# One level of Strassen in the first product of an MLP, for groups 2 to 7 of 8

## The reference, cut to what matters

```
h = layer_norm(DEEPNORM_ALPHA * h + mixed @ w_out, ln1_g, ln1_b)
f = jnp.square(jax.nn.relu(h @ w_ff1)) @ w_ff2        # w_ff1: 1024 x 4096, w_ff2: 4096 x 1024
h = layer_norm(DEEPNORM_ALPHA * h + f, ln2_g, ln2_b)
```

## Time and profile before

| | |
|---|---|
| median of 3 runs | 698.24 us (698.01 to 699.11) |
| the profiled execution | 697.22 us, its span 695.4 us |
| granted TensorE clock, mean | 0.997 |
| busy share of the span | TensorE 98%, VectorE 52%, GpSimd 49%, ScalarE 38% |
| the MLP's groups from up 1 to down 6 | 321.4 to 657.4 us of the span |

### The profile page before, as it was taken

The page is one execution under the profiler, slowest core; times in us unless marked ns, Lnnn a source line. Parts: engine busy times, 40 slices in busy tenths (PEclk is TensorE's granted clock), DMA queues, the critical chain, the costliest instruction groups (busy, mean ns, idle before and its releaser), DMA issues.

```text
span 695.4 us, 13894 instructions
## 1 busy us (share of the span) xinstructions
PE 682.0 (98%) x5643; PEld 656.1 (94%) x5643; DVE 362.9 (52%) x710; ACT 265.4 (38%) x512; POOL 341.1 (49%) x438
## 2 busy tenths in 40 slices
PE   8999999999999999999999999999999999999996
PEld 5989999999997589999999999999999999999995
DVE  7745646576655546589633524525325335245246
ACT  6866666777656334552222112212112112122112
POOL 4554233444444034407964645545545556455437
PEclk9999999999999999999999999999999999999998
DMA  7362231321448922102232222222222222322303
GB/s 242 100 213 73 82 92 61 91 84 49 137 165 278 345 75 92 62 32 91 90 124 78 83 94 82 91 91 92 91 91 89 95 65 88 94 90 91 122 1 129
DMA packets 34005, 73.66 MB, mean 106 GB/s; under 512 B 3988, under 2 KB 19380, under 8 KB 33942
## 3 DMA queue, kind: packets, MB, share of 16 engines
q1 hardware_dynamic: 26822, 68.88, 30.1%
q10 hardware_dynamic: 6864, 3.90, 1.9%
q0 software_dynamic: 256, 0.00, 0.0%
HBM read 67.16 MB, written 5.60 MB: 105 GB/s over the span
## 4 chain that ended last, share of the span: by engine, by line
PE 89%; DVE 3%; ACT 2%; DMA 2%; SPq 2%; issue 1%; POOL 0%; ACTq 0%; DVEq 0%
PE acc L2000 48%; PE acc L1639 29%; PE o_bank L1747 2%; PE acc L1733 1%; PE t_bank L1733 1%; DMA k_t<-cache_k_b 1%; DMA xin<-x_prompt 1%; PE acc L1763 1%; ACT xin L752 1%; SPq L542 1%; PE s_bank L1723 1%; DMA w_raw<-weights 1%; PE s_bank L1722 1%; PE s_bank L1719 0%; PE s_bank L1720 0%
## 5 line engine op out<-in xcount | busy, mean ns | idle before, releaser
L629 POOL TENSOR_TENSOR w_lo<-w_raw,w_hi 128x256 fp32r<-128x256 f32 x352 | 280.2, 827 | 301.4 <-ACT w_hi L731 301.4
L731 ACT ACTIVATE w_hi<-w_raw 128x1024 fp32r<-128x1024 f32 x88 | 92.9, 1057 | 161.1 <-PE acc L2000 132.5
L1639 PE MATMUL acc<-h_hi,w_hi 128*128 128x288 f32 (+1 forms) x416 | 129.2, 311 | 1.7 <-DVE h_lo L1142 1.1
L1639 PE MATMUL acc<-h_lo,w_hi 128*128 128x288 f32 (+1 forms) x416 | 119.6, 288 | 0.0
L1639 PE MATMUL acc<-h_hi,w_lo 128*128 128x288 f32 (+1 forms) x416 | 119.5, 287 | 0.0
L1564 DVE TENSOR_TENSOR res<-res,acc 128x256 f32<-128x256 f32 x112 | 43.9, 433 | 104.2 <-PE acc L2000 104.2
L2000 PE MATMUL acc<-h_hi,w_lo 128*128 128x256 f32 x448 | 92.3, 288 | 0.0
L2000 PE MATMUL acc<-m_hi,w_lo 128*128 128x256 f32 x448 | 92.3, 288 | 0.0
L2000 PE MATMUL acc<-m_hi,w_hi 128*128 128x256 f32 x448 | 92.3, 287 | 0.0
L2000 PE MATMUL acc<-h_hi,w_hi 128*128 128x256 f32 x448 | 92.3, 287 | 0.0
L2000 PE MATMUL acc<-h_lo,w_hi 128*128 128x256 f32 x448 | 92.2, 287 | 0.0
(11 more groups left out here) (280 smaller groups left out, 1121.0 us busy)
## 6 DMA issues: line engine op xcount, KB each, us to landing
w_raw<-weights SPq DMA_DIRECT2D x94, 512.0 KB, 3.4
k_t<-cache_k_a SPq DMA_DIRECT2D x16, 192.0 KB, 4.1
k_t<-cache_k_b SPq DMA_DIRECT2D x16, 192.0 KB, 4.2
v_pg<-cache_v_a SPq DMA_DIRECT2D x8, 192.0 KB, 4.2
v_pg<-cache_v_b SPq DMA_DIRECT2D x8, 192.0 KB, 4.2
k_t<-cache_v_b SPq DMA_DIRECT2D x8, 192.0 KB, 4.4
y_prompt<-y_n SPq DMA_DIRECT2D x6, 256.0 KB, 2.1
xin<-x_prompt SPq DMA_DIRECT2D x4, 256.0 KB, 3.8
```

What stands on the lines that cost most here:

```text
L629: op = pool.tensor_tensor(w_lo[:, slot, part], w_raw[:, stage, part], w_hi[:, slot, part].bitcast(F32), ALU.subtract)
L731: act.activation(w_hi[:, slot, :], w_raw[:, stage, :], ACT.Copy).then_inc(hi_done, 1)
L1639: mm = pe.matmul(out, w[:, slot, cols(k)], x[:, ks[k], halves(hf)], start=(fresh and k == 0 and pas == 0), stop=last)
```

## The change

For groups 2 to 7 the first product is taken in pairs of tiles. A pair's weights form a 2 x 2 block matrix (two tiles by two halves of the 8 k tiles), and so does the data (two halves of k by two halves of 272 tokens, `LEFT` and `RIGHT`). Seven block products with sums of blocks give the four result blocks (Winograd's form of Strassen's scheme).

- Data: four sums of blocks of `res` (4 k tiles x 272), made by VectorE in up 1 (`t_add`), copied to high parts by ScalarE (`t_high`) and reduced to low parts by VectorE (`t_rest`). The fourth replaces the `RIGHT` blocks of the upper half in `h_hi`, `h_lo`. GpSimd now only adds the bias to `res`; the scale is part of the first group's residual adds.
- Weights: four sums of 128 x 512 a pair on VectorE (`s_sums`). High and low parts are made for "parts" of 512 columns, 22 a round (14 for two pairs, 8 for the second product), in a ring of 11 (`part_at`). `w_raw` has four buffers (`w_raw`, `w_raw2`).
- A round is up of group t+2 and down of group t+1; there are `ROUNDS` = 6, then "last". TensorE: 14 products of 12 matmuls of 272 columns, in six banks, then 8 m's as before.
- VectorE puts the seven products together with adds (`rounds`), and squares with relu in one instruction; the high part of the hidden layer is now copied by ScalarE (`hidden_high`), the low part stays on VectorE (`hidden_rest`).

The diff, cut to its core:

```diff
+            def rounds():            # TensorE
+                pe.wait_ge(norm1_lo, 2 * KT + 4)
+                for t in range(ROUNDS):
+                    for p in range(2):
+                        n = 2 * t + p
+                        for q in range(PRODUCTS):
+                            i = PARTS * t + PRODUCTS * p + q
+                            pe.wait_ge(part_lo, i + 1)
...
+                            up_product(n, q, i)
+                    pe.wait_ge(hid_lo_done, FG * (STRASSEN + t))
+                    for m in range(DOWNS):
+                        i = PARTS * t + 2 * PRODUCTS + 2 * (m // 2)
+                        pe.wait_ge(part_lo, i + 2)
+                        if m == 1:
+                            pe.wait_ge(up_added, 7 * n + 4)
+                        if m >= 2:
+                            pe.wait_ge(acc_dve, DOWN0 + 2 * DOWNS * t + 2 * (m - 1))
+                        down_parts(i, m % 2, (STRASSEN + t - 1) % 2, 2 * (m % 2))
```

```diff
             # VectorE, group 1 (up), behind each tile j
+                        if j == 0:
+                            dve.wait_ge(res_shifted, KT)
+                            t_add(t_sum0, res[:, 0:KT // 2, RIGHT], res[:, 0:KT // 2, LEFT])
+                            dve.wait_ge(t_summed, 1)
+                            t_add(t_sum1, res[:, KT // 2:KT, RIGHT], t_sum0[:, :, :])
+                        if j == 1:
+                            t_add(t_sum2, res[:, KT // 2:KT, RIGHT], res[:, 0:KT // 2, RIGHT])
+                        if j == 2:
+                            t_rest(0, t_sum0, t_hi[:, 0, :, :], t_lo[:, 0, :, :])
+                            t_rest(1, t_sum1, t_hi[:, 1, :, :], t_lo[:, 1, :, :])
+                            dve.wait_ge(t_summed, 2)
+                            dve.wait_ge(norm1_lo, 2 * KT + 1)
+                            t_add(t_sum0, res[:, KT // 2:KT, LEFT], t_sum1[:, :, :])
+                        if j == 3:
+                            t_rest(2, t_sum2, t_hi[:, 2, :, :], t_lo[:, 2, :, :])
             # VectorE, group 0 (down)
-                            if c["down"] == 0 and hf == 0:
-                                dve.wait_ge(res_scaled, m + 1)
-                            dve.tensor_tensor(res[:, m, halves(hf)], res[:, m, halves(hf)],
-                                              acc[:, 2 * (m % 2) + hf, 0:WIDE[hf]], ALU.add).then_inc(acc_dve, 1)
+                            dve.scalar_tensor_tensor(res[:, m, halves(hf)], res[:, m, halves(hf)], ALPHA,
+                                                     acc[:, 2 * (m % 2) + hf, 0:WIDE[hf]], ALU.mult,
+                                                     ALU.add).then_inc(acc_dve, 1)
+                        if m == 0:
+                            t_rest(3, t_sum0, h_hi[:, 0:KT // 2, RIGHT], h_lo[:, 0:KT // 2, RIGHT])
+                        if m == 2:
+                            s_sums(0)
+                        if m == 6:
+                            s_sums(1)
```

```diff
+            def s_sums(n):           # VectorE, four sums of 128 x 512
+                t, p = divmod(n, 2)
+                v = 2 * FG * t + 2 * p
+                if n:
+                    dve.wait_ge(part_lo, PARTS * ((n - 1) // 2) + PRODUCTS * ((n - 1) % 2) + 5)
+                dve.wait_ge(*raw_sem(v))
+                dve.wait_ge(*raw_sem(v + 1))
...
+            def rounds():            # VectorE
+                for t in range(ROUNDS):
+                    for p in range(2):
+                        n = 2 * t + p
+                        step, x = HALF0 + STEPS * t + PRODUCTS * p, PRODUCTS * p
+                        p1, p5, u2, u3 = (kept[:, p, r, :] for r in range(4))
+                        dve.wait_ge(half_done, step + 3)
+                        dve.wait_ge(up_kept, 2 * n + 2)
+                        dve.tensor_tensor(u2, up_bank(x + 2), p1, ALU.add).then_inc(up_added, 1)
+                        if p:
+                            hidden_rest(n - 1)
...
+                    if t + 1 < ROUNDS:
+                        s_sums(2 * t + 2)
+                    for m in range(DOWNS):
+                        for hf in range(2):
+                            dve.wait_ge(half_done, HALF0 + STEPS * t + 2 * PRODUCTS + 2 * m + hf + 1)
+                            dve.tensor_tensor(res[:, m, halves(hf)], res[:, m, halves(hf)],
+                                              acc[:, 2 * (m % 2) + hf, 0:WIDE[hf]], ALU.add).then_inc(acc_dve, 1)
+                        if m == 2:
+                            hidden_rest(n)
+                        if m == 4 and t + 1 < ROUNDS:
+                            s_sums(2 * t + 3)
```

```diff
+            def rounds():            # GpSimd
+                for i in range(ALL_PARTS):
+                    hi, lo = part_at(i)
+                    src, _ = part_from(i)
+                    pool.wait_ge(part_hi, i + 1)
+                    for a in range(0, PART, 2 * P):
+                        cols = slice(a, a + 2 * P)
+                        op = pool.tensor_tensor(lo[:, cols], src[:, cols], hi[:, cols].bitcast(F32), ALU.subtract)
+                    op.then_inc(part_lo, 1)
+            def rounds():            # SyncE, the loads
+                for v in range(2 * FG * ROUNDS + FG):
+                    if v == 0:
+                        sp.wait_ge(t_summed, 4)
+                        sp.wait_ge(norm1_lo, 2 * KT + 3)
+                    if v in (2, 3):
+                        sp.wait_ge(lo_done, FF0 + 3 * FG + v - 3)
+                    if v >= 4:
+                        sp.wait_ge(part_lo, raw_free(v - 4))
+                    sp.dma_start(raw_at(v), weights[FF0 + 3 * FG + v]).then_inc(raw_sem(v)[0], 16)
```

More of the change, by code:

```diff
@@ L479, in mlp @@
             c = run({"unit": FF0, "tile": FF0, "act": ACT0, "dve": DVE0, "up": 0, "down": 0}, MLP_HEAD)
-            for i in range(MLP_ROUNDS):
-                run({k: i * (2 * up[k] + 2 * down[k]) + c[k] for k in c}, MLP_BODY)
-            run({k: c[k] + MLP_ROUNDS * (2 * up[k] + 2 * down[k]) for k in c}, MLP_TAIL)
+            rounds()
+            run({"unit": c["unit"] + 2 * FG * ROUNDS, "tile": c["tile"] + ROUNDS * STEPS // 2, "act": c["act"],
+                 "dve": c["dve"] + ROUNDS * 2 * DOWNS, "up": NG, "down": NG - 1}, MLP_TAIL)
@@ L1061, in segment @@
                     relu_half(3, c)
-                for j in range(FG):
-                    if kind == "up" and prev is not None:
+                    for j in range(FG):
+                        hi_part((FF0 + j) % RING, (FF0 + j) % STAGE, c["unit"] + j + RING, c["tile"] * 2 + j + 1 + UPS,
+                                c["unit"] * (16 // STAGE) + 16 * ((j + RING) // STAGE + 1))
+                elif kind == "up":
+                    for j in range(FG):
                         act.wait_ge(half_done, (c["tile"] + j) * 2 + 1)
@@ L1067, in segment @@
                                        ACT.Relu).then_inc(acc_act, 1)
[L1068 to L1076, removed]
@@ L1077, in _ @@
-            mlp(act, segment)
+                        hi_part((FF0 + j) % RING, (FF0 + j) % STAGE, c["unit"] + j + RING, c["tile"] * 2 + 2 * (j + 1),
+                                c["unit"] * (16 // STAGE) + 16 * ((j + RING) // STAGE + 1))
+                        if j == 1:
+                            t_high(0, t_sum0, t_hi[:, 0, :, :])
+                            t_high(1, t_sum1, t_hi[:, 1, :, :])
+                        if j == 2:
+                            t_high(2, t_sum2, t_hi[:, 2, :, :])
+                elif kind == "down":
+                    act.wait_ge(half_done, HALF0 - 2 * DOWNS)
+                    t_high(3, t_sum0, h_hi[:, 0:KT // 2, RIGHT])
+                    for i in range(len(W_AT)):
+                        part_high(i)
@@ L1080, in _ @@
+            mlp(act, segment, rounds)
             for o in range(QT + 1):
@@ L1588, in _ @@
+            mlp(dve, segment, rounds)
             norm2_stats(3, 1)
@@ L1602, in _ @@
             norm2_finish(4, 1, 2)
[L1603 removed]
+            dve.wait_ge(y_dve_done, 4)
         @block.tensor
@@ new lines, in down_parts @@
+            def down_parts(i, mj, par, at):
+                for f in range(FG):
+                    cols = slice(2 * P * (f % 2) + P * mj, 2 * P * (f % 2) + P * (mj + 1))
+                    whi, wlo = part_at(i + f // 2)
+                    for pas in range(3):
+                        last = f == FG - 1 and pas == 2
+                        for hf in range(2):
+                            mm = pe.matmul(acc[:, at + hf, 0:WIDE[hf]], (whi, whi, wlo)[pas][:, cols],
+                                           (m_hi, m_lo, m_hi)[pas][:, FG * par + f, halves(hf)],
+                                           start=(f == 0 and pas == 0), stop=last)
+                            if last:
+                                mm.then_inc(half_done, 1)
@@ new lines, in up_product @@
+            def up_product(n, q, i):
+                out = up_bank(PRODUCTS * (n % 2) + q)
+                whi, wlo = part_at(i)
```

(7 more changed lines are left out.)

263 lines of the change are left out of this document (225 added, 38 removed).

## The result

The changed kernel takes **706.0 us** (median of 4; 705.1 to 708.5) beside 698.4 for the kernel before in the same comparison: ratio 1.0114, 95% interval 1.0087 to 1.0141. It is slower by 8 us, outside the range of the prediction (686.5 to 703.5). The profiled execution took 706.22 us with a span of 704.4, 9.0 more than before.

The account below looks back on a forecast made before the run. TensorE, busy 98% of the span, was taken as the bound at 125 ns a matmul. Saving -17.2, head +8.4 and rounds +6.0 sum to -2.8 us: 695.4 us, own range 691 to 699.5, eight in ten 686.5 to 703.5.

Parts of the forecast that it names:

- the head's first: Groups 1 and 0: after tile 0 VectorE waits for eight GpSimd shifts of the residual, 8.14 us, ending at 338.2.
- the first difference: In the head, VectorE's first block difference of the residual, 1088 elements, takes 1.7 us while GpSimd runs.
- The saving: Groups 2 to 7: 1008 matmuls of 272 columns at 125.8 ns replace 1152 at 125.0, -17.2 us.
- Rival 2: Products run at the wide form's pace: saving only 10.0, same waits, +4.4, 702.6 us; chance 0.08.
- The rounds: Four contended sums ahead of m=0's residual adds make TensorE wait 1.2 us before m=2 in five rounds, +6.0 us.
- Adds of VectorE: VectorE adds of two SBUF tensors: 1088 elements 1.30 us free, 1.71 beside GpSimd; 512 elements 0.70 and 1.11.
- Rival 1: The adds are cheap, mostly meeting a quiet GpSimd: head +6.0, no wait in the rounds, -11.2, 687.0 us; chance 0.18.
- Rival 3: VectorE and GpSimd take strict turns, a 0.71 us block before each SBUF add: +4.2, 702.4 us; chance 0.22.
- GpSimd, ScalarE and loads in the rounds at nothing: In each round the work of GpSimd and ScalarE and the weight loads cost TensorE 0.
- Rival 4: GpSimd is the bound: above 1.05 us a block it outlasts a round; at 1.13, 716 us; chance 0.05.
- The head's last term: End of the head: first four weight sums delay m=3's residual adds, 0.3 us behind when m=5 wants its banks.
- Clock: Head: TensorE may lose clock after its waits, 0 to 1.9 us; taken as 0.

Follow-up runs that it names:

- experiments 3 to 6: In order: changed kernel with weight sums cut (1.0008); with GpSimd held for the first difference (1.0048); unedited again (1.0104); kernel before with one-operation shift (1.0059).
- experiment 1: Changed kernel with the residual shift on GpSimd in two operations again (add, then multiply by 1.0): ratio 0.9983 to the kernel before.
- the repeat: The changed kernel timed and profiled once more with no edit, fifth of the follow-up runs: ratio 1.0104 to the kernel before.
- experiment 10: Changed kernel with two edits, residual shift on ScalarE and each round's weight sums cut around m=0's residual adds: ratio 0.9841 to the kernel before, 688.75 us.
- Experiment 3: Changed kernel with two of each round's four weight sums moved behind the residual adds of m=0: ratio 1.0008 to the kernel before.
- experiment 6: Kernel before, no Strassen, with the one-operation shift on GpSimd and the scale in group 0's residual adds: ratio 1.0059, 4.1 us slower.
- experiment 2: Changed kernel with the residual shift moved from GpSimd to ScalarE: ratio 0.9918 to the kernel before.
- experiment 8: Changed kernel with shift on ScalarE, sums cut, group 1's relus earlier and three low parts behind group 0's residual adds: ratio 0.9824 to the kernel before.

## Why the prediction was wrong

**The step that failed** is the head's first: "it waits for all eight shifts of the residual on GpSimd, which end at 330.03 + 8.14 = 338.2". The 8.14 is a row of another instruction. The change drops the multiplication, I took the shorter form to cost no more than the longer, and said nothing of it. With one operation eight shifts took 13.4 to 13.9 us in all five profiled executions that have it (the profile after, experiments 3 to 6, the last being the old kernel with only that edit), and 6.7 with the second operation restored (experiment 1). Counted from group 1's start, the shifts ended 23.3 us in, where I had 17.1: +6.2, of which 5.4 are their duration and the rest a later start.

**The second miss** is the first difference: 1.7 forecast, 6.58 in the profile after, +4.9. The head's 18.2 less the 8.4 forecast is 9.8; 6.2 + 4.9 is 11.1. Up to the relu of tile 3 VectorE made up 2.8 of it, where its instructions met an idle GpSimd (1.28 a difference instead of the 1.7 forecast). Behind that relu it lost 1.4 again, where GpSimd still ran: the rest of tile 3 and a low part took 4.6 and not 3.2. In the repeat the difference took 1.80, as forecast. There the head's 8.8 over the forecast are 5.6 of late shifts, 1.4 behind the relu of tile 3, 1.5 of clock and 0.3 in small terms.

Over the whole span the forecast was 11.8 us short (-2.8 against +9.0): 9.8 in the head, 0.9 in the rounds (1.2 more of waits, 0.3 more saved), and 1.1 outside both.

**Point by point:**
- *The saving*: 6 x (21.09 + 24.0) = 270.5 us in experiment 10, which has no waits in the rounds, against 288.0: -17.5, forecast -17.2. A 272-column matmul is 125.5 ns, forecast 125.8. Rival 2 (wide-form pace) is refuted.
- *The rounds*: waits of 1.2 us forecast in front of m=2, five times. TensorE lost 277.7 - 270.5 = 7.2, 1.4 each (6.1 of it as waits), for the reason given: four contended sums of 1.12 to 1.23 ahead of the adds. Experiment 3 removes the order alone, and the wait goes.
- *Adds of VectorE*: 1088 elements take 1.28 free and 1.82 beside GpSimd (forecast 1.30 and 1.71), 512 take 0.69 and 1.12 to 1.23 (0.70 and 1.11). Rival 1 (the adds are cheap) is refuted by the rounds.
- *Rival 3 (strict turns)*: right in its sign, wrong in its place and price. The rounds lose 1.4 and not 2.3, and a contended add costs 0.5 us more, less than a whole block of 0.71. Nor does a block's turn give the long form of the first difference, which came behind eight. The slowdown that this rival forecast came from somewhere else.
- *GpSimd, ScalarE and loads in the rounds at nothing*: right, no wait names them. Rival 4 is refuted: the period is 46.4 us, and GpSimd keeps up with it.
- *The head's last term*: by the forecast's own steps it is 0.7 and not 0.3 (m=3's adds end at 368.3 + 0.85, m=5 wants its banks at 359.4 + 9.0). From m=2 on the head of the profile after lost 0.1.
- *Clock*: taken as 0, end 1.9. In the profile after that held. Its stretches, columns as in the earlier trace rows:
```profile
345.00:350.00 5.00, 0.00 (x0) 0.00 (x0) 4.60 (x1) 0.00 (x0) 5.00 (x8) 0.54 0.16 30
...
355.00:360.00 5.00, 5.00 (x27) 5.00 (x26) 4.81 (x6) 1.78 (x2) 4.25 (x4) 0.60 0.01 2
360.00:365.00 5.00, 5.00 (x43) 5.00 (x42) 4.90 (x6) 1.87 (x3) 2.10 (x3) 1.00 0.00 0
```
  The slow matmuls of tile 3 and m=0 weren't what m=2 waited for: 144 matmuls from 370.23 took 18.32 us, 127 ns each. It is no rule: in the repeat and in experiment 1 the wait in front of m=2 (2.1 us) cost 1.5 us of clock. In the repaired kernels, where VectorE is early, more of it comes onto the path (2.9 us in experiment 10, past my end).

Had the shift kept its price, the forecast would have stood near the mark, in part by luck: experiment 1, which is the change with that one repair, has the ratio 0.9983 (0.9957 to 1.001), and the forecast's -2.8 us is 0.996. But its head is 12.8 us over the old one and not 8.4, with the long difference and 1.5 us of clock in it.

**What stays open.** Why a difference that starts 0.05 to 0.08 us behind GpSimd's run sometimes takes as long as all eight blocks and itself (6.58 in the profile after, 6.61 in experiment 1) and sometimes shares with them (1.80, experiments 3 and 5) was not settled. The Trainium skill (SBUF — State Buffer, "SBUF: two separate sides") says that whoever starts first has the shared port pair for its whole instruction. That fits neither form whole: in 6.58 us the difference stood behind eight instructions, and 1.80 is 0.52 more than the free 1.28, less than a block of 0.69, though blocks run all the while. Why the one-operation form is slow, and why group 1 starts up to 4.7 us later in some executions, are open too.

## What to carry to other kernels

Take a duration from a row of the same instruction form: an operation less can cost twice the time, and work that hides behind an idle stretch shows its price only when a busy engine is made to wait for it. When a change puts new work into a full queue, look first at which instruction frees another engine's buffer and what stands ahead of it; cutting a block of four sums in two was worth 1% at no cost. And a repair that leaves short waits on TensorE can pay again in clock, so count waits and clock together. Where the profile names no releaser for a wait, look in the program for what it waits for (experiment 6).

## What the runs showed of the hardware

- GpSimd's tensor_scalar on 128 x 544 fp32 with a per-partition operand: 1.64 us with one operation, 0.73 (here, quiet) to 1.05 us (before, beside VectorE) with two. ScalarE does the same addition in 0.74 (experiment 2).
- An add of two SBUF tensors on VectorE that started 0.05 us behind eight GpSimd blocks took 6.58 us and the blocks 5.49 (0.69 each) in one execution; 0.07 us behind them it took 1.80 and the blocks 10.40 (1.30 each) in another of the same program.
- A TensorE wait of 3.0 us in the middle of a stretch at full clock was followed by a granted clock of 0.50 from 354 to 360 us (experiment 10), and one of 1.9 us by 0.57 over 4 us (experiment 8). Waits of 2.4, 1.6 and 0.7 us within 12 us left it at 1.00 (experiment 6). So the length of one wait didn't tell what it would cost.
